# Prompt attention: compressed scores beside small jobs, another order of maxima, low parts and outputs

## The reference, cut to what matters

```python
p_c = masked_softmax(jnp.einsum('bqkgd,bnkd->bqkgn', q, kc) * scale, m_c)   # 63 compressed blocks
o_c = jnp.einsum('bqkgn,bnkd->bqkgd', p_c.astype(vc.dtype), vc)
...
p_s = masked_softmax(jnp.einsum('bqkgd,bkqmd->bqkgm', q, ks) * scale, m_s)  # selected blocks: all of them
p_w = masked_softmax(jnp.einsum('bqkgd,bwkd->bqkgw', q, kw) * scale, m_w)   # window of 512
return gates[..., 0:1] * o_c + gates[..., 1:2] * o_s + gates[..., 2:3] * o_w
```

## Time and profile before

| | us |
|---|---|
| median of three runs | 2128.96 |
| the profiled execution | 2132.16 |
| its span | 2130.4 |
| TensorE busy | 1948.7 |
| VectorE busy | 1075.2 |
| ScalarE busy | 869.0 |
| GpSimd busy | 473.3 |

### The profile page before, as it was taken

How to read it: one execution, slowest core, us unless ns; L and a number is a source line. 1 busy time by engine, 2 the same in 40 slices (tenths; PEclk the granted TensorE clock), 3 DMA queues, 4 the chain that set the end, 5 groups by cost and what they waited for, 6 DMA issues and landing times. The chain is left out here.

```text
span 2130.4 us, 31355 instructions
## 1 busy us (share of the span) xinstructions
PE 1948.7 (91%) x11570; PEld 1737.3 (82%) x11571; DVE 1075.2 (50%) x1525; ACT 869.0 (41%) x1451; POOL 473.3 (22%) x640
## 2 busy tenths in 40 slices
PE   7989999999999978888888888989994899999996
PEld 6869999999989867777778777789883788888883
DVE  5442211100112347677767767754447568654655
ACT  3002211112110346666666766731001367554654
POOL 0000000000000223444444443300221135322333
PEclk9989999999999969999999999999997899999998
DMA  5011111132213400000000000052433489867764
GB/s 208 1 30 40 40 50 50 40 123 80 77 45 80 129 11 1 1 1 1 1 1 2 1 1 1 1 168 60 170 143 146 175 287 400 295 220 274 288 236 169
DMA packets 98516, 215.65 MB, mean 101 GB/s; under 512 B 23130, under 2 KB 71810, under 8 KB 92226
## 3 DMA queue, kind: packets, MB, share of 16 engines
q1 hardware_dynamic: 90946, 188.90, 24.6%
q0 software_dynamic: 7456, 25.17, 4.7%
HBM read 181.88 MB, written 34.26 MB: 101 GB/s over the span
## 5 line engine op out<-in xcount | busy, mean ns | idle before, releaser
L1569 DVE TENSOR_TENSOR turned_low<-ps,turned_high 128x512 fp32r<-128x512 f32 (+2 forms) x304 | 186.9, 618 | 86.9 <-ACT turned_high L1646 83.5
L1440 PE MATMUL ps<-key_stacks,query_stacks 128*128 128x256 f32 (+3 forms) x384 | 146.2, 381 | 52.7 <-ACT small L1626 27.5
L1646 ACT CAST turned_high<-ps 128x512 fp32r<-128x512 f32 (+2 forms) x304 | 156.7, 525 | 85.1 <-PE ps L1465 84.6
L1545 DVE TENSOR_REDUCE small<-ps 128x1 f32<-128x640 f32 (+7 forms) x256 | 178.4, 697 | 17.1 <-PE ps L1432 16.3
L1699 POOL TENSOR_SCALAR region_w<-region_w,small,gates 128x640 f32<-128x640 f32 (+7 forms) x172 | 132.7, 781 | 229.2 <-DVE small L1549 229.2
L1486 PE MATMUL ps<-turned_high,value_stacks 128*128 128x256 f32 (+1 forms) x608 | 160.5, 297 | 11.9 <-DVE region L1577 11.3
L1635 ACT ACTIVATE region_w<-ps,small 128x640 f32<-128x640 f32 (+7 forms) x172 | 120.4, 700 | 72.1 <-DVE small L1545 64.8
L1486 PE MATMUL ps<-turned_low,value_stacks 128*128 128x256 f32 (+1 forms) x608 | 149.7, 290 | 0.0
L2386 PE MATMUL ps<-gate_parts,rows_parts 128*128 128x512 f32 x576 | 140.2, 400 | 4.1 <-DVE rows_parts L2680 4.1
L2386 PE MATMUL ps<-down_parts,hidden_parts 128*128 128x512 f32 x576 | 139.3, 399 | 1.8 <-issue 1.4
L1440 PEld LDWEIGHTS ps<-key_stacks,query_stacks 128*128 128x128 f32 x384 | 75.4, 196 | 77.4 <-issue 73.2
(11 more groups left out here) (448 smaller groups left out, 5025.9 us busy)
## 6 DMA issues: line engine op xcount, KB each, us to landing
region_k<-in_w_gate SPq DMA_DIRECT2D x16, 2048.0 KB, 9.2
region_k<-in_w_up SPq DMA_DIRECT2D x16, 2048.0 KB, 10.1
region_w<-in_w_down SPq DMA_DIRECT2D x16, 2048.0 KB, 12.8
region_w<-in_w_in SPq DMA_DIRECT2D x20, 512.0 KB, 3.7
gate_b<-region_w SPq DMA_DIRECT2D x8, 516.0 KB, 4.0
region_w<-gate_b SPq DMA_DIRECT2D x8, 516.0 KB, 3.8
region_k<-in_x_prompt SPq DMA_DIRECT2D x8, 512.0 KB, 6.7
region_w<-in_w_in SPq DMA_DIRECT2D x4, 1024.0 KB, 14.4
```

What stands on the lines that cost most here:

```text
L1440: nc.tensor.matmul(out, qs[:, g, tile], k1[:, a, g, k0:k0 + w], start=True, stop=False, skip_group_check=True)
L1545: nc.vector.tensor_reduce(nmax[:, n % 4:n % 4 + 1], sc, AX.X, ALU.max, negate=True).then_inc(s_max, 1)
L1569: nc.vector.tensor_tensor(lo, m.ps[:, turn_bank(G), 0:w], hi, ALU.subtract).then_inc(s_lo, 1)
L1646: nc.scalar.copy(hi, m.ps[:, turn_bank(G), 0:w]).then_inc(s_hi, 1)
```

## The change

- The compressed job is no longer one of the jobs. Its scores go to the second bank of the slot of job (H, 0), with H % 16 = 0 or 4 (widths 128 and 384, which need one bank only), right behind that job's scores. It has semaphores of its own for scores, differences and exponential. The scores of job (H + 1, 0), which take the same slot, also wait for its differences. Its turn stays where it was.
- In VectorE's round the first maximum comes first, then the compressed maximum, reciprocals, output, compressed gain, the second maximum, and then all low parts.
- In ScalarE's round the compressed exponential stands behind the second high part and the second exponential behind the third.
- The output of a tile pair is copied and added in the round with H % 4 = 1 (H from 5 on), ScalarE's part first in the round, VectorE's behind the reciprocals; the last one after the loop.

```diff
     def compressed_ahead(H):
-        return H % 8 == 0 and H < NHALF
+        return H % 16 in (0, 4) and H < NHALF
+
+    def compressed_of(H):
+        return 2 * (H // 16) + (H % 16) // 4
...
     for H in range(NHALF):
-        if compressed_ahead(H):
-            jobs.append(("C", H // 8))
         jobs += [(H, 0), (H, 1)]
...
+    def compressed_bank(c):
+        return scores_bank(n_of[16 * (c // 2) + 4 * (c % 2), 0]) + 1
...
             def free_scores(n):
                 if n >= 2:
                     pe.wait_ge(s_exp, n - 1)
+                    H, t = jobs[n - 2]
+                    if t == 0 and compressed_ahead(H):
+                        pe.wait_ge(s_cd, compressed_of(H) + 1)
 
             def compressed_scores(c):
 
-                n = n_of["C", c]
-                bank = scores_bank(n)
+                bank = compressed_bank(c)
                 pe.wait_ge(s_q, 4 * (c // 2) + 2 * (c % 2) + 2)
-                free_scores(n)
...
             # TensorE's round
                 if H + 2 < NHALF:
-                    if compressed_ahead(H + 2):
-                        compressed_scores((H + 2) // 8)
                     scores(H + 2, 0)
+                if H + 2 < NHALF and compressed_ahead(H + 2):
+                    compressed_scores(compressed_of(H + 2))
...
             # VectorE's round
+                if H + 2 < NHALF:
+                    job_max(H + 2, 0)
+                if H + 2 < NHALF and compressed_ahead(H + 2):
+                    compressed_max(compressed_of(H + 2))
                 if 0 <= H + 1 < NHALF:
                     reciprocals(H + 1)
-                    if compressed_ahead(H + 1):
-                        compressed_gain((H + 1) // 8)
                 if H == 1:
                     dve.wait_ge(s_vl, 4)
+                if H >= 5 and H % 4 == 1:
+                    output(H // 4 - 1)
+                if 0 <= H + 1 < NHALF and compressed_ahead(H + 1):
+                    compressed_gain(compressed_of(H + 1))
                 if H + 2 < NHALF:
-                    if compressed_ahead(H + 2):
-                        compressed_max((H + 2) // 8)
-                    job_max(H + 2, 0)
+                    job_max(H + 2, 1)
                 for G in todo[0:1]:
                     low(G)
-                if H + 2 < NHALF:
-                    job_max(H + 2, 1)
-                for G in todo[1:3]:
+                for G in todo[1:2]:
                     low(G)
-                if H >= 4 and H % 4 == 0:
-                    output(H // 4 - 1)
+                for G in todo[2:3]:
+                    low(G)
...
             # ScalarE's round
+                if H >= 5 and H % 4 == 1:
+                    output_half(H // 4 - 1)
                 for G in todo[0:1]:
                     high(G)
                 if H + 2 < NHALF:
-                    if compressed_ahead(H + 2):
-                        compressed_probs((H + 2) // 8)
                     job_probs(H + 2, 0)
                 for G in todo[1:2]:
                     high(G)
+                if H + 2 < NHALF and compressed_ahead(H + 2):
+                    compressed_probs(compressed_of(H + 2))
+                for G in todo[2:3]:
+                    high(G)
                 if H + 2 < NHALF:
                     job_probs(H + 2, 1)
-                for G in todo[2:3]:
-                    high(G)
-                if H >= 4 and H % 4 == 0:
-                    output_half(H // 4 - 1)
...
+            output_half(NHALF // 4 - 1)
```

More of the change, by code:

```diff
@@ L1329, in attend_prompt @@
         if compressed_ahead(H):
-            scaled.append(("C", H // 8))
+            scaled.append(("C", compressed_of(H)))
     n_of = {job: n for n, job in enumerate(jobs)}
@@ L1371, in attend_prompt @@
     s_cmax, s_csum, s_cgain = m.sem("a_c_max"), m.sem("a_c_sum"), m.sem("a_c_gain")
+    s_cs, s_cd, s_cp = (m.sem("a_c_" + n) for n in ("scores", "differences", "probs"))
     s_t, s_hi, s_lo = m.sem("a_turned"), m.sem("a_turned_high"), m.sem("a_turned_low")
@@ L1420, in compressed_scores @@
                                                 skip_group_check=True)
-                last.then_inc(s_qk, 1)
+                last.then_inc(s_cs, 1)
             def scores(H, t):
@@ L1505, in _ @@
                     scores(H + 2, 1)
-                for G in todo[1:3]:
+                for G in todo[1:2]:
+                    turn(G)
+                for G in todo[2:3]:
                     turn(G)
@@ L1522, in compressed_max @@
             def compressed_max(c):
-                n, q = n_of["C", c], c % 2
-                sc = m.ps[:, scores_bank(n), :].rearrange("p (x n) -> p x n", n=64)[:, :, 0:NCMP]
-                dve.wait_ge(s_qk, n + 1)
+                q = c % 2
+                sc = m.ps[:, compressed_bank(c), :].rearrange("p (x n) -> p x n", n=64)[:, :, 0:NCMP]
+                dve.wait_ge(s_cs, c + 1)
                 done = 3 * (c // 2) + 2 * q
@@ L1537, in compressed_max @@
                 nc.vector.tensor_tensor(pc_rows[:, 8 * q:8 * q + 8, 0:NCMP], sc,
-                                        cmax.unsqueeze(2).to_broadcast([P, 8, NCMP]), ALU.add).then_inc(s_max, 1)
+                                        cmax.unsqueeze(2).to_broadcast([P, 8, NCMP]), ALU.add).then_inc(s_cd, 1)
             def job_max(H, t):
@@ L1553, in compressed_gain @@
                 done = 5 * j + 3 * q
-                dve.wait_ge(s_exp, n_of["C", c] + 1)
+                dve.wait_ge(s_cp, c + 1)
                 nc.vector.tensor_reduce(csum[q], pc_rows[:, 8 * q:8 * q + 8, 0:NCMP], AX.X, ALU.add).then_inc(s_csum, 1)
@@ L1607, in _ @@
                         low_queries_at_first(p)
+            output(NHALF // 4 - 1)
         @block.scalar
@@ L1624, in compressed_probs @@
                 x = pc_rows[:, 8 * (c % 2):8 * (c % 2) + 8, 0:NCMP]
-                act.wait_ge(s_max, n_of["C", c] + 1)
-                nc.scalar.activation(x, x, ACT.Exp).then_inc(s_exp, 1)
+                act.wait_ge(s_cd, c + 1)
+                nc.scalar.activation(x, x, ACT.Exp).then_inc(s_cp, 1)
             def job_probs(H, t):
@@ L1725, in _ @@
                     if compressed_ahead(H + 1):
-                        compressed_scale((H + 1) // 8)
+                        compressed_scale(compressed_of(H + 1))
                 if H == -1:
```

## The result

The kernel after takes 2031.17 us (median, 2030.77 to 2032.07), the kernel before 2127.56 us in the same runs: ratio 0.9559, interval [0.9526, 0.9593]. That is 96 us less; the forecast was 57 less (2072 us, range 2048 to 2106).

The account below looks back on a forecast made before the run. TensorE, busy 91% of the span, was taken as the bound, idle 9.4 us a head. Terms -22.5 - 20 - 8 + 5 - 8 = -53.5 gave 2075 us; 3 us of drain made it 2072, range 2048 to 2106.

Parts of the forecast that it names:

- Compressed scores in the spare bank: Prompt attention: TensorE's 27.5 us of waits for the compressed exponential go, 5 us charged for the odd job; -22.5 us.
- The clock: Seven passages from head to head in attention return to full clock, 2.9 us each; -20 us (bounds 0 and -24).
- the first rival: The clock keeps falling, or falls elsewhere in the head; waits go but not the -20: 2092 us, chance 0.16.
- Maxima ahead of low parts: VectorE's round: earlier maxima remove a third of 24.6 us of score waits for ordinary exponentials; -8 us (bounds +8, -24.6).
- the drain: TensorE: where idle time goes, the drain ahead is overlapped too; 0.1 us at each of 16 + 16 places, 3 us less.
- Low parts later: VectorE's low parts, behind the second maximum, delay transposes' banks and values: +5 us on 7.8 (bounds -8 and +25).
- ScalarE's second exponential: Behind the third high part on ScalarE, 0.58 us later in halves of 10 or more blocks; nothing (bounds 0 and +5).
- The output a half later: Tile pair's output copies and additions: values' 11.3 us of waits fall to 3; -8 us (bounds -11 and +8).
- The reciprocals start GpSimd's scaling later: Attention: scaling starts later by 2 us plus the maximum in the passage, transposes a round later; nothing.
- The four rivals: Whole change: clock falls on 2092 us (0.16), traded waits 2103 (0.10), does not do what it says 2124 (0.05), slower 2260 (0.05).

## Why the prediction was wrong in size

- *Compressed scores in the spare bank* (-22.5, and its share of the clock). The mechanism was right: the waits of the earlier trace rows for L1626 are gone, 1.1 us came in their place where I had charged 5. The spare bank alone measured 35, of which 27 are idle time.
- *The clock* (-20). Right in cause at the passages: putting the wait back brings falls back (0.93), filling it takes them away (0.98). Near in size: the stage lost some 37 us of clock and some 10 are left, so 27. The seven passages account for the 20 by my own sum; the rest is chiefly the first head's fall of 11 us, which I left as it was and which went. Right by luck in one point: I gave the term to the spare bank, and with the bank and the old orders the falls only move to the odd compressed job (0.96 for the stage), as the first rival said. The new orders were needed to end them.
- *Maxima ahead of low parts* (-8, "a third of 24.6"). This is the step that failed: the share of the slot waits that VectorE's order makes. It measured 21.4 us of the waits themselves, and 25 us of time. The third was a choice between bounds 33 us apart. The row that I went by, 17.8 us of reciprocals waiting, is the smaller part in time: undoing that order costs 4 us, the low part between the maxima 21. I named that low part and gave it no number. It is the largest waiting term that was short, by 13 us, but not the only one: the next term and the drain were short by 12 and 15.
- *Low parts later* (+5). Wrong sign: the waits of transposes for them fell from 7.8 to 0.4. The cause is not in this term but in the output's: only with the output in its old place do they come back (9.1 us). Putting the low parts behind both maxima cost the transposes nothing that a trace shows.
- *ScalarE's second exponential* (nothing). Right beside the other new orders (2 us), wrong beside the old ones (21).
- *The output a half later* (-8, by shorter waits of the values). Wrong reason: these waits are 10.5 us, hardly shorter. The step is worth 15 us because VectorE no longer stands still at it with the low parts and maxima behind it; that the 8 I took is about half of it is chance.
- *The reciprocals start GpSimd's scaling later* (nothing). 5.9 us of new waits.
- *Drain* (-3). Some 18 us of busy time went that I can put down to nothing else. That they are drain is not shown. I counted 32 places; the earlier trace rows has 114 of TensorE's waits.
- *The range*. The good ends of my own bounds (-27.5, -24, -24.6, -8, -11) add to 95 us, which is 2034 us from the profiled execution less 3.2. I stopped at 2048 with all of the slot waits gone (and 8 us of these were already in the forecast, so that end itself should have been near 2055). The four rivals all lay on the slow side, and the case that came, every small term at its good end together, was none of them. It is one case and not five in part, because the same in-order queue on VectorE made several of these waits. That the sum comes so near the measured 96 is luck all the same: it holds 11 us of waits for the output, of which 10.5 stayed, and not the 18 above.
- The rule of the Trainium skill that I set against the clock term ("TensorE: Matmul & The Clock Gate"; it stands in the section behind the one I named, "A second HAM failure mode: psum-queue depth-cycling": short idle times between groups of matmuls send the clock to and fro) describes the spare bank alone better than I allowed: five heads fall among the small jobs. It did not hold against the change, whose head runs at 1.00. The short idle times went there as well, which fits the rule; no run filled them while keeping the old orders.

## What to carry to other kernels

In a slot loop over several in-order engines, ask for each instruction what it waits for *and* what stands behind it: an operation whose wait ends late (here the low part, which waits for another engine's high part) belongs behind everything that is ready earlier and that the bound engine needs. Waits with one common cause go together, so their good ends have to be added in the range. A wait can be worth more than its idle time: 16 compressed waits cost 27 us of idle time here and 24 more by the clock. And a fall of the clock that a change takes from one place can turn up in another, so look at the clock of the whole stage. The price of an order undone alone may be far too low: one step cost 2 us alone and 21 with the others.

## What was not expected of the hardware

Eight useless matmuls in an idle stretch made the kernel before 10 us faster and the kernel with the wait put back 18 us faster, by the granted clock (0.94 to 0.97, and 0.93 to 0.98). And the fall is not tied to the place of a long wait: with the spare bank alone TensorE went to 1.2 GHz within 2 us of the start of an odd compressed job, in five heads, with no wait for a compressed exponential left. Why the other three heads escaped was not tried.
